# Norm2 interleaved with the out-projection, residual loaded in place, inverse root by Ln and Exp (hybrid decoder block)

## What is computed

```
mix = concat([rms_norm(y_conv, conv_out_g), rms_norm(y_attn, attn_out_g)])
x = x + gate1 * (mix @ w_out)
h2 = modulate(rms_norm(x, norm2_g), shift2, scale2)
f = square(relu(h2 @ w_ff1)) @ w_ff2
x = x + gate2 * f
```

## Time and profile before

| what | us |
|---|---|
| median of 2 runs, slowest core | 1301.02 (1299.56 to 1302.48) |
| profiled execution, device time | 1300.66 |
| its span on core 0, the slowest | 1299.1 |
| spans of the eight cores | 1283.7 to 1299.1 |
| busy on core 0: PE, DVE, ACT | 1066.0, 659.5, 627.4 |

### The profile page before, as it was taken

One profiled execution on the slowest core, in us unless ns is written; L12 is line 12 of the kernel. 1 busy time (PEld: TensorE's weight loads), 2 busy tenths in 40 slices (PEclk: granted clock), 3 DMA queues, 4 the chain that ended last, 5 costly groups with the idle time before them and its releaser, 6 DMA issues.

```text
span 1299.1 us, 19255 instructions; the slowest of 8 cores (1283.7 to 1299.1 us)
## 1 busy us (share of the span) xinstructions
PE 1066.0 (82%) x5430; PEld 474.2 (37%) x5528; DVE 659.5 (51%) x935; ACT 627.4 (48%) x950; POOL 33.2 (3%) x44
## 2 busy tenths in 40 slices
PE   0137978898889788887888595769999999999998
PEld 0123433334334334423332242334444444444443
DVE  0132145655555645553334684344666555665557
ACT  1275267887798777896889003542111111111120
POOL 0102000000000000000000000000000000000000
PEclk9998989998999989997999696888999999999999
DMA  9935562022022020031200546200123033000113
GB/s 179 185 114 67 56 89 33 1 33 34 1 34 34 1 33 1 2 66 49 81 1 1 132 161 120 44 0 2 20 46 66 1 66 58 8 1 1 66 65 130
DMA packets 42295, 67.61 MB, mean 52 GB/s; under 512 B 9936, under 2 KB 26576, under 8 KB 42192
## 3 DMA queue, kind: packets, MB, share of 16 engines
q0 software_dynamic: 33408, 35.65, 18.6%
q1 hardware_dynamic: 8784, 30.72, 6.8%
HBM read 93.63 MB, written 8.39 MB: 79 GB/s over the span
## 4 chain that ended last, share of the span: by engine, by line
PE 68%; ACT 13%; issue 7%; DVE 6%; DMA 5%; ACTq 0%; DVEq 0%; POOL 0%; POOLq 0%; SPq 0%
PE ps L285 67%; ACT arena L288 12%; DMA arena<-w_ada 3%; DMA arena<-w_in 1%; ACT small L288 1%; PE ps L390 1%; DVE arena L382 1%; DVE arena L733 1%; DMA arena<-x 1%; DVE arena L826 1%; DVE arena L720 1%; DVE arena L638 1%; DVE arena L734 0%; DVE arena L576 0%; DVE arena L398 0%
## 5 line engine op out<-in xcount | busy, mean ns | idle before, releaser
L285 PE MATMUL ps<-arena 128*128 128x512 bf16 (+5 forms) x3830 | 840.9, 377 | 59.2 <-DVE arena L638 14.3
L288 ACT ACTIVATE arena<-ps 128x1024 f32<-128x1024 f32 (+5 forms) x512 | 384.2, 761 | 462.3 <-PE ps L285 450.8
L285 PEld LDWEIGHTS ps<-arena 128*128 128x128 bf16 (+2 forms) x3904 | 359.7, 100 | 516.0 <-issue 196.3
L720 DVE TENSOR_TENSOR arena<-arena 128x1024 bf16<-128x1024 f32 (+3 forms) x160 | 170.2, 1064 | 195.7 <-PE ps L285 103.0
L288 ACT ACTIVATE arena<-arena 128x1024 bf16<-128x1024 f32 (+5 forms) x248 | 206.1, 831 | 106.5 <-DVE arena L845 70.2
L285 PE MATMUL ps<-arena,cbf_sb 128*128 128x512 bf16 (+3 forms) x642 | 162.3, 355 | 35.3 <-ACT arena L288 32.9
L889 DVE TENSOR_TENSOR arena<-arena 128x512 bf16<-128x512 f32 x128 | 88.6, 692 | 128.4 <-ACT arena L288 128.0
L904 DVE TENSOR_TENSOR arena<-ps,gate_b 128x512 f32<-128x512 f32 x128 | 88.6, 692 | 31.2 <-PE ps L285 31.1
L285 PEld LDWEIGHTS ps<-arena,cbf_sb 128*128 128x128 bf16 x664 | 58.6, 101 | 112.9 <-issue 93.0
L907 DVE TENSOR_TENSOR arena<-arena 128x512 f32<-128x512 f32 x128 | 88.6, 692 | 13.7 <-DVE arena L904 0.5
L390 PE MATMUL ps<-cbf_sb,arena 128*128 128x128 bf16 x256 | 30.5, 270 | 60.3 <-ACT arena L288 36.9
(11 more groups left out here) (42 smaller groups left out, 225.3 us busy)
## 6 DMA issues: line engine op xcount, KB each, us to landing
arena<-x SPq DMA_DIRECT2D x32, 512.0 KB, 4.1
arena<-w_ff POOLq DMA_DIRECT2D x16, 1024.0 KB, 8.3
arena<-w_ada POOLq DMA_DIRECT2D x12, 1024.0 KB, 9.4
out<-arena SPq DMA_DIRECT2D x16, 512.0 KB, 2.6
arena<-w_in POOLq DMA_DIRECT2D x4, 1024.0 KB, 14.7
arena<-w_out SPq DMA_DIRECT2D x8, 512.0 KB, 3.3
arena<-w_in POOLq DMA_DIRECT2D x8, 256.0 KB, 22.7
arena<-b_ada SPq DMA_DIRECT2D x1, 512.0 KB, 11.1
```

The costliest lines, as they stand in the source:

```text
L285: return op("pe", lambda e: e.matmul(out, lhsT=lhsT, rhs=rhs, start=start, stop=stop, **kw), reads, writes)
L288: return op("act", lambda e: e.activation(out=out, in_=in_, func=func, **kw), reads, writes)
L720: op("dve", lambda e, n=n, qlo=qlo: e.tensor_tensor(out=a_v[n % 2][:, :, qlo:512], in0=u_v[n % 3][:, :, qlo:512], in1=r_v[:, :, qlo:512], ...
```

## The change

The inverse root of the mixers' sums is made by two ScalarE operations (Ln straight from PSUM, with 1/512 as scale and EPS as bias, then Exp with scale -0.5). `wog` becomes eight buffers. The residual is loaded by SP into `x1` itself, all sixteen blocks ahead of the out-projection, blocks 8 to 15 first. Norm2's buffers and functions are made before the out-projection, and n2_stats and n2_transp are written into its loop, one group behind; only n2_transp(3) is left for the MLP, after its first ffn1.

```diff
-    op("dve", lambda e: e.tensor_scalar(out=small[:, SM_TMP:SM_TMP + 32], in0=bank(PSTAT)[:, 0:32], scalar1=1.0 / 512, scalar2=EPS,
-                                        op0=ALU.mult, op1=ALU.add), [bankb[PSTAT]], [b_small["tmp"]])
-    act(small[:, SM_TMP2:SM_TMP2 + 32], small[:, SM_TMP:SM_TMP + 32], AF.Sqrt, [b_small["tmp"]], [b_small["tmp2"]])
-    op("dve", lambda e: e.reciprocal(out=small[:, SM_RSM:SM_RSM + 32], in_=small[:, SM_TMP2:SM_TMP2 + 32]), [b_small["tmp2"]], [b_small["rsm"]])
+    act(small[:, SM_TMP2:SM_TMP2 + 32], bank(PSTAT)[:, 0:32], AF.Ln, [bankb[PSTAT], b_eps], [b_small["tmp2"]],
+        scale=1.0 / 512, bias=small[:, SM_EPS:SM_EPS + 1])
+    act(small[:, SM_RSM:SM_RSM + 32], small[:, SM_TMP2:SM_TMP2 + 32], AF.Exp, [b_small["tmp2"]], [b_small["rsm"]], scale=-0.5)
     wog_v, wog_r = view(96 * KB, [128, 8, D], BF16)
-    wog_b = abuf("wog", wog_r)
+    wog_b = abufs(["wog%d" % kc for kc in range(8)], wog_r)
     for kc in range(8):
...
-                                                          in1=g1b_v, op0=ALU.mult, op1=ALU.mult), [wo32_b, b_vecs, b_g1b], [wog_b])
-    xs2_v, xs2_b = [], []
-    for i in range(2):
-        v_, r_ = view((176 + 4 * i) * KB, [128, D], F32)
-        xs2_v.append(v_)
-        xs2_b.append(abuf("xs2_%d" % i, r_))
+                                                          in1=g1b_v, op0=ALU.mult, op1=ALU.mult), [wo32_b, b_vecs, b_g1b], [wog_b[kc]])
     x1_v, x1_r = view(0, [128, NTB, D], F32)
     x1_b = [abuf("x1_%d" % tb, (tb * 4 * KB, (tb + 1) * 4 * KB)) for tb in range(NTB)]
+    h2T_v, h2T_r = view(64 * KB, [128, 8, S], BF16)
+    h2T_b = abufs(["h2T%d" % tg for tg in range(NTT)], h2T_r)
+    xn2_v, xn2_r = view(176 * KB, [128, 4, D], BF16)
+    xn2_b = abuf("xn2", xn2_r)
+    n2_stats, n2_transp = make_norm(2, h2T_v, h2T_b, lambda tb: (x1_v[:, tb, :], x1_b[tb]), [xn2_v], [xn2_b],
+                                    lambda tg, tbi: (xn2_v[:, tbi, :], xn2_b))
+    for tb in list(range(8, NTB)) + list(range(8)):
+        dma("sp", x1_v[:, tb, :], x_d[tb * 128:(tb + 1) * 128, :], writes=[x1_b[tb]])
     for tb in range(NTB):
-        i = tb % 2
-        dma("sp", xs2_v[i], x_d[tb * 128:(tb + 1) * 128, :], writes=[xs2_b[i]])
...
-            op("dve", lambda e, dst=dst, bc=bc, tb=tb, i=i, fh=fh: e.scalar_tensor_tensor(
-                out=dst, in0=bank(bc), scalar=small[:, SM_RSM + tb:SM_RSM + tb + 1], in1=xs2_v[i][:, fh * 512:(fh + 1) * 512],
-                op0=ALU.mult, op1=ALU.add), [bankb[bc], b_small["rsm"], xs2_b[i]], [x1_b[tb]])
+            op("dve", lambda e, dst=dst, bc=bc, tb=tb: e.scalar_tensor_tensor(
+                out=dst, in0=bank(bc), scalar=small[:, SM_RSM + tb:SM_RSM + tb + 1], in1=dst,
+                op0=ALU.mult, op1=ALU.add), [bankb[bc], b_small["rsm"], x1_b[tb]], [x1_b[tb]])
...
+        if tb == 3:
+            n2_stats(0)
+        elif tb == 7:
+            n2_transp(0, banks=(6, 7))
+            n2_stats(1)
+        elif tb == 11:
+            n2_transp(1, banks=(6, 7))
+            n2_stats(2)
+        elif tb == 15:
+            n2_transp(2, banks=(6, 7))
+            n2_stats(3)
...
-    n2_stats(0)
-    n2_transp(0, banks=(6, 7))
-    n2_stats(1)
     for s_, (qtr, tt) in enumerate(steps):
         ffn1(qtr, tt)
-        if qtr == 0 and tt + 1 < NTT:
-            n2_transp(tt + 1, banks=(6, 7))
-            if tt + 2 < NTT:
-                n2_stats(tt + 2)
+        if s_ == 0:
+            n2_transp(3, banks=(6, 7))
```

More of the change, by code:

```diff
@@ L840, in build @@
             for j in range(4):
-                mm(bank(bc), yc_v[:, j, tb * 128:(tb + 1) * 128], wog_v[:, j, fh * 512:(fh + 1) * 512], j == 0, j == 3, [yc_b, wog_b], [bankb[bc]])
+                mm(bank(bc), yc_v[:, j, tb * 128:(tb + 1) * 128], wog_v[:, j, fh * 512:(fh + 1) * 512], j == 0, j == 3, [yc_b, wog_b[j]], [bankb[bc]])
             for c in range(4):
-                mm(bank(ba), ya_v[:, c, tb * 128:(tb + 1) * 128], wog_v[:, 4 + c, fh * 512:(fh + 1) * 512], c == 0, c == 3, ya_b + [wog_b], [bankb[ba]])
+                mm(bank(ba), ya_v[:, c, tb * 128:(tb + 1) * 128], wog_v[:, 4 + c, fh * 512:(fh + 1) * 512], c == 0, c == 3, ya_b + [wog_b[4 + c]], [bankb[ba]])
             dst = x1_v[:, tb, fh * 512:(fh + 1) * 512]
-            op("dve", lambda e, dst=dst, bc=bc, tb=tb, i=i, fh=fh: e.scalar_tensor_tensor(
-                out=dst, in0=bank(bc), scalar=small[:, SM_RSM + tb:SM_RSM + tb + 1], in1=xs2_v[i][:, fh * 512:(fh + 1) * 512],
-                op0=ALU.mult, op1=ALU.add), [bankb[bc], b_small["rsm"], xs2_b[i]], [x1_b[tb]])
+            op("dve", lambda e, dst=dst, bc=bc, tb=tb: e.scalar_tensor_tensor(
+                out=dst, in0=bank(bc), scalar=small[:, SM_RSM + tb:SM_RSM + tb + 1], in1=dst,
+                op0=ALU.mult, op1=ALU.add), [bankb[bc], b_small["rsm"], x1_b[tb]], [x1_b[tb]])
             op("dve", lambda e, dst=dst, ba=ba, tb=tb: e.scalar_tensor_tensor(
@@ L856, in build @@
         return finish()
[L858 to L861, removed]
     ffw[1] = load_ffn_weights(1, 1)
-    n2_stats, n2_transp = make_norm(2, h2T_v, h2T_b, lambda tb: (x1_v[:, tb, :], x1_b[tb]), [xn2_v], [xn2_b],
-                                    lambda tg, tbi: (xn2_v[:, tbi, :], xn2_b))
     gT_v, gT_b = [], []
```

## The result

The changed kernel takes 1307.76 us (median of 13 runs) against 1299.96 (12 runs of the kernel before, same comparison). All ratios leave out the executions in which the cores of a die ran at a lower clock; the ratio here is 1.0053, interval 1.0039 to 1.0067: slower by 0.5%, about 7 us, and clear of no change. 1312 was forecast, 11 us above the 1300.66 from which the sum started.

What follows compares the result with a forecast made beforehand. Out-projection paced by DVE as much as PE, without slack. First FFN matmul 34.5 us later (start +4.9, DVE's waits and norm work 47.1, restarts 4.0, less 20.4 and 1.0), FFN 23 less: 1300.66 + 11.5 = 1312, range 1296 to 1328.

Steps and rivals of the forecast that it cites:

- A: The forecast itself, whole kernel: slower, 1312 us, own range 1303 to 1321, chance 0.66.
- First load: Start of the out-projection: the first evacuation waits for residual block 0, third in SP's queue, until 739.5 us (732 to 743).
- Scalings: Start, w_out's eight scalings on DVE: they start at 717.1, come 1.39 us apart and end at 728.1.
- Out-projection on DVE: Evacuations, statistics and transposes in DVE's order from 739.5: 102.4 us, to 841.9, or 845.9 with restarts.
- the first statistics: Out-projection, norm2's first group on DVE: 0.75 plus three steps of 2.79 us and two gaps, 9.3 us.
- a restart: Out-projection: PE returns at half clock after each of four stops, 1.0 us each (0 if covered, 2.65 if not).
- MLP: The FFN stage: PE ends at 1305.9 us against 1294.35 before, +11.5, with an unchanged tail.
- The stop for Relu: Start of the FFN: Relu stands behind ScalarE's last statistics until 856.7 us, with 24 matmuls done.
- the two slow stretches: FFN: PE runs at half clock twice, 2.65 us of loss each, 5.3 in all.
- B: Rival, out-projection: PE does not regain full clock and becomes the bound, +25 us, 1337, chance 0.14.
- C: Rival: residual block 0 lands at 732.3 and restarts cost nothing, also in the FFN; 1295.5 us, chance 0.12.
- D: Rival, out-projection: interleaving hides, DVE pays only its own work; 1279 us, 1.6% faster (2.2% with early load), chance 0.08.

Runs made afterwards that it cites:

- The first experiment: The changed kernel with its block groups worked in order 2, 3, 0, 1, in out-projection and MLP, against the kernel before: 1293.27 us, ratio 0.9967.

## Why the prediction was right, and by how much it was off

The sign came out, and by the steps given: the case that held was A. The size was too large: 11.3 us were forecast against 1300.66, and about 7 measured; 1312 was 4 us too high. The prediction took 2% for the least that can be told from no change; the interval here is 0.14% to either side.

- **First load.** The wait from the last scaling to the first evacuation was put at 11.2 us (728.3 to 739.5). The median over cores is 11.2, and the ends given, 732 and 743, hold all but the slowest core, whose wait was 15.0. The mechanism was right, but that the number is met exactly is luck: 739.5 was chosen between a sum of 737.5 and a row that gave 743 (it is nearer to the first, not to the row as the prediction says), and the cores lie between 7.3 and 15.0.
- **Scalings.** Mis-sized: 1.39 us each was taken from the row of before; it is 1.19. The old spacing held a wait of DVE for itself, on the shared buffer, that the split removes. 1.5 us too high.
- **Out-projection on DVE.** 105.8 us from the first evacuation to the first MLP matmul were forecast, 104.6 measured (740.56 to 845.14): 9.0 for the first statistics (9.3), 5.1 for a round of transposes (5.5), 10.2 for the statistics behind it (10.65), and 15.0 for sixteen evacuations after a stop, so 1.2 for a restart (1.0).
- **MLP.** The stop for Relu ends 11.2 us after the start (11.4). From there to the last matmul 449.2 were forecast and 446.7 measured (856.34 to just ahead of the last evacuation at 1303.10). This was the largest error behind the first evacuation, 2.5 us, in two halves: the round of transposes took 5.8 instead of 7.1, and the two slow stretches 4.0 instead of 5.3 (40 matmuls in 10.40 us, 118 in 27.67, against 0.2158 each).

```profile
872.58 27.67 PE L285 MATMUL ps<-arena 128*128 128x512 bf16 x118
```

- **Cores.** The sum was made on one core. As a tail it forecasts 594.8 us (a span of 1310.6, less the 715.8 at which the last L733 starts). Core 2 of the changed kernel has 593.0, 1.8 less, but only because its first load took 3.8 us longer than the sum had it, which hid most of the errors above. The median core has 587.6, 7.2 less, of which 1.7 lie ahead of the first evacuation. The core of before that the sum started from had a tail 1.7 us longer than the median. The +6.1 of the median core and the 0.53% of the slowest agree within their spread.
- **B (PE stays at half clock)** did not occur: the first stretch of 64 matmuls took 16.69 us, 13.8 at full clock and 2.9 of loss, and the same in the next ones (13.2 for 48, of which 10.4 would be full clock), much as after the stop in the earlier trace rows, where twelve matmuls lost 2.7.
- **C (small gain)** needed a fast load and free restarts, and had neither: a restart in the out-projection cost 1.2 us and the two in the MLP 4.0. The first experiment comes near C's number (1293.3, C 1295.5) because it takes the wait for the load away altogether, with the restarts still paid. **D (hiding)** failed on the chain between ScalarE and DVE, which came 2.79 us apart as in the earlier trace rows. With that chain cut and the load gone the change gave 1.9%, near D's 1.6 to 2.2%.

## What to carry to other kernels

Work moved beside other work is only hidden if the engine that carries the host stage does not have to wait for it: here DVE paced the out-projection and stood in order behind a chain through ScalarE, so 3 us of its work cost 9. Look for the scratch output that shares a buffer with a real one, and for a load whose target is freed by the last step before it is needed: splitting the one and reordering the blocks around the other turned +0.5% into -1.9% with the same arithmetic. After that, cut the guest work into small pieces between the host's steps: the last version did so, together with moving the scaling to ScalarE, and came to -4.6%.

## What was not expected of the hardware

DVE operations that write to one buffer and wait for each other by semaphore are 1.39 us apart here, the same operations without that wait 1.19, though each lasts about 1.27 (10.2 us of busy time for the eight of before): without the wait the next begins before the last has ended.

And a load is delayed by what was issued ahead of it, in its own queue or in another, and not by what is issued behind it. A load of 512 KB lands in 3.0 to 4.8 us when alone, and in 3.3 to 4.9 with nine more right behind it and POOL's queue empty. With 1 MB issued on POOL's queue 1.6 to 2.1 us ahead it took 7.4 to 8.6. The kernel with block 0 first has cores of both kinds, which is why its waits lie between 4.4 and 8.8. The grouping is read from the traces; no run moved POOL's issue by a microsecond or two and nothing else.
